# Attention scores of the mixing stage: one accumulation group a head, one mask product, rounded log-gate products of 384 columns

## The reference, cut to what matters

```python
# differential, per 128-query block
s = einsum('bqhcd,bkhcd->bhcqk', qi, k) * scale
p = softmax(where(causal, s, NEG_INF))
a = p[:, :, 0] - lam * p[:, :, 1]
# forgetting: logit[t,s] = q_t.k_s/sqrt(d) + sum_{s<j<=t} log f_j, causal
cum = cumsum(log_f, axis=1)
s = einsum('bqhd,bkhd->bhqk', qi, k) * scale + ci[..., None] - cum_k[:, :, None, :]
p = softmax(where(causal, s, NEG_INF))
```

## Time and profile before

| | |
|---|---|
| time, median of 3 runs | 2051.53 us (2051.78, 2051.53, 2048.94) |
| the profiled execution | 2050.4 us |
| its span, first to last instruction | 2048.3 us |
| TensorE busy | 1985.8 us (97%) |
| VectorE busy | 1429.2 us (70%) |
| ScalarE busy | 1147.7 us (56%) |
| mean granted TensorE clock | 0.993 |

### The profile page before, as it was taken

How to read it: one execution, slowest core, us unless ns; L and a number is a source line. 1 busy time by engine, 2 the same in 40 slices (tenths; PEclk the granted TensorE clock), 3 DMA queues, 4 the chain that set the end, 5 groups by cost and what they waited for, 6 DMA issues and landing times.

```text
span 2048.3 us, 33381 instructions
## 1 busy us (share of the span) xinstructions
PE 1985.8 (97%) x13864; PEld 1799.4 (88%) x13864; DVE 1429.2 (70%) x1902; ACT 1147.7 (56%) x1811; POOL 42.6 (2%) x32
## 2 busy tenths in 40 slices
PE   7999999999999999999999999999999999999999
PEld 7898798888989888888799987889989998878998
DVE  5456698898445778988856578765566657876555
ACT  6358745455435865554655565665565556566554
POOL 0100000000010000000001000000000100000000
PEclk9999999999999999999999999999999999999999
DMA  7353267996544236999555543245546554334553
GB/s 285 124 206 106 101 258 297 382 389 256 188 179 147 104 124 242 384 393 375 189 202 185 185 158 111 103 167 187 187 153 209 186 184 164 124 107 161 185 185 124
DMA packets 56165, 409.56 MB, mean 200 GB/s; under 512 B 6608, under 2 KB 6992, under 8 KB 7888
## 3 DMA queue, kind: packets, MB, share of 16 engines
q1 hardware_dynamic: 46512, 330.23, 45.2%
q10 hardware_dynamic: 9504, 77.21, 9.4%
HBM read 406.37 MB, written 1.05 MB: 199 GB/s over the span
## 4 chain that ended last, share of the span: by engine, by line
PE 81%; DVE 11%; ACT 5%; issue 2%; DMA 0%; POOL 0%; DVEq 0%; ACTq 0%; SPq 0%; POOLq 0%
PE bank L567 25%; PE bank L568 25%; PE bank L569 25%; DVE weights_low L392 3%; ACT weights_high L381 1%; DVE work L2311 1%; PE bank L949 1%; ACT weights_high L382 1%; PE bank L1906 1%; DVE work L523 1%; DVE h_low L534 1%; DVE work L1506 0%; DVE scratch L1501 0%; ACT work L435 0%; ACT work L436 0%
## 5 line engine op out<-in xcount | busy, mean ns | idle before, releaser
L392 DVE TENSOR_TENSOR weights_low<-raw_weights,weights_high 128x1024 fp32r<-128x1024 f32 x608 | 725.7, 1234 | 386.2 <-ACT weights_high L381 384.1
L567 PE MATMUL bank<-h_high,weights_high 128*128 128x256 f32 x3024 | 869.1, 287 | 17.6 <-DVE h_low L534 10.8
L568 PE MATMUL bank<-h_low,weights_high 128*128 128x256 f32 x3024 | 857.5, 284 | 0.0
L569 PE MATMUL bank<-h_high,weights_low 128*128 128x256 f32 x3024 | 857.2, 283 | 0.0
L381 ACT ACTIVATE weights_high<-raw_weights 128x1024 fp32r<-128x1024 f32 x304 | 321.6, 1058 | 631.3 <-PE bank L569 593.4
L567 PEld LDWEIGHTS bank<-h_high,weights_high 128*128 128x128 f32 x3024 | 581.6, 192 | 40.7 <-issue 17.0
L568 PEld LDWEIGHTS bank<-h_low,weights_high 128*128 128x128 f32 x3024 | 581.9, 192 | 2.6 <-issue 0.5
L569 PEld LDWEIGHTS bank<-h_high,weights_low 128*128 128x128 f32 x3024 | 581.8, 192 | 0.0
L382 ACT ACTIVATE weights_high<-raw_weights 128x1024 fp32r<-128x1024 f32 x304 | 317.5, 1044 | 0.0
L567 PE MATMUL bank<-weights_high,hidden_high 128*128 128x512 f32 x640 | 251.3, 393 | 1.8 <-DVE weights_low L392 1.8
L568 PE MATMUL bank<-weights_low,hidden_high 128*128 128x512 f32 x640 | 249.8, 390 | 0.0
(11 more groups left out here) (300 smaller groups left out, 1883.7 us busy)
## 6 DMA issues: line engine op xcount, KB each, us to landing
raw_weights<-in_stream SPq DMA_DIRECT2D x310, 1024.0 KB, 4.9
work<-in_ada ACTq DMA_DIRECT2D x64, 1152.0 KB, 9.2
consts<-in_consts SPq DMA_DIRECT2D x1, 2048.0 KB, 12.6
work<-in_row ACTq DMA_DIRECT2D x2, 836.0 KB, 5.1
x<-in_x SPq DMA_DIRECT2D x1, 1024.0 KB, 5.1
out_x<-x SPq DMA_DIRECT2D x4, 256.0 KB, 2.0
gain_row<-in_final SPq DMA_DIRECT2D x1, 512.0 KB, 13.2
vec<-in_vec SPq DMA_DIRECT2D x1, 169.0 KB, 12.5
```

The source lines that it names most:

```text
L392: dve.tensor_tensor(low[:, c], raw[:, c], high[:, c].bitcast(F32), ALU.subtract).then_inc(m.raw_done[plan.index[name] % RAW], 1)
L567: pe.matmul(out, aH, bH, start=start, stop=False, skip_group_check=True)
L568: pe.matmul(out, aH, bL, start=False, stop=False, skip_group_check=True)
L569: return pe.matmul(out, aL, bH, start=False, stop=stop, skip_group_check=True)
```

## The change

`mask_r` grows from two to five blocks of 128 columns; ScalarE fills the new three at the start with rounded copies of `tri_le`, `tri_le` and `ones`, both of which hold only 0 and 1. A new tensor `fox_r` of 16 columns holds the log gates as a rounded high part (8 columns) and a rounded low part (8 columns), written by two new VectorE instructions behind the one that used to signal `fox_lf`.

In `scores`, the product for the first block alone starts an accumulation; the q·k product of the second block follows at once and adds. The log gates of a fox task are added by four rounded products: for the high and then the low part, one of 384 columns (triangle, triangle, ones) and one of 128 columns. One rounded mask product per task covers both diagonal blocks (256 columns, every other block of 128 of the bank).

```diff
-        self.mask_r = sb("mask_rounded", 2 * P, F32R)
+        self.mask_r = sb("mask_rounded", 5 * P, F32R)
+        self.fox_r = sb("fox_rounded", 16, F32R)
...
-        def gate(i, tt):
-            return cols(m, FOX_LF + 4 * tt + i - FOX).to_broadcast([P, P])
+        def gate(i, tt, low):
+            at = 8 * low + 4 * tt + i - FOX
+            return m.fox_r[:, at:at + 1].to_broadcast([P, P])
 
         for i in tasks:
             q, k = qk(i)
             pe.matmul(score_bank(m, i)[:, 0:128], q[:, 0:128], k[:, 0:128], start=True, stop=False, skip_group_check=True)
+        for i in tasks:
+            q, k = qk(i)
+            add(score_bank(m, i)[:, 128:384], q[:, 128:256], k[:, 0:256])
         if first >= FOX:
             for i in tasks:
-                add(score_bank(m, i)[:, 0:128], gate(i, 0), m.const("tri_le"))
+                for low in range(2):
+                    add(score_bank(m, i), gate(i, 0, low), m.mask_r[:, 2 * P:5 * P])
+                    add(score_bank(m, i)[:, 256:384], gate(i, 1, low), m.mask_r[:, 2 * P:3 * P])
         for i in tasks:
-            add(score_bank(m, i)[:, 0:128], m.mask_r[:, 0:P], m.mask_r[:, P:2 * P], True)
-        for i in tasks:
-            q, k = qk(i)
-            pe.matmul(score_bank(m, i)[:, 128:384], q[:, 128:256], k[:, 0:256], start=True, stop=False, skip_group_check=True)
-        if first >= FOX:
-            for i in tasks:
-                s = score_bank(m, i)
-                add(s[:, 128:256], gate(i, 0), m.const("tri_le"), True)
-                add(s[:, 256:384], gate(i, 0), m.const("ones"))
-                add(s[:, 256:384], gate(i, 1), m.const("tri_le"))
-        for i in tasks:
-            add(score_bank(m, i)[:, 256:384], m.mask_r[:, 0:P], m.mask_r[:, P:2 * P], True).then_inc(m["scored"], 1)
+            add(tiles(score_bank(m, i), 3)[:, 0::2], m.mask_r[:, 0:P], wide(m.mask_r[:, P:2 * P], 2), True).then_inc(m["scored"], 1)
...
             dve.wait_ge(m["fox_l"], m.at("fox_l", 1))
-            dve.tensor_tensor(cols(m, FOX_LF, 8), cols(m, FOX_LF, 8), cols(m, FOX_L, 8), ALU.add).then_inc(m["fox_lf"], 1)
+            step(dve.tensor_tensor(cols(m, FOX_LF, 8), cols(m, FOX_LF, 8), cols(m, FOX_L, 8), ALU.add))
+            step(dve.tensor_copy(m.fox_r[:, 0:8], cols(m, FOX_LF, 8)))
+            dve.tensor_tensor(m.fox_r[:, 8:16], cols(m, FOX_LF, 8), m.fox_r[:, 0:8].bitcast(F32), ALU.subtract).then_inc(m["fox_lf"], 1)
             at_event(split_low, dve, m, plan, "ff")
...
+    for b, name in enumerate(("tri_le", "tri_le", "ones")):
+        act.activation(m.mask_r[:, (2 + b) * P:(3 + b) * P], m.const(name), ACT.Copy)
```

## The result

The changed kernel takes 2040.01 us (median of 5 runs, 2038.92 to 2041.27) against 2049.95 us for the kernel before (5 runs, 2048.94 to 2051.78): a ratio of 0.995, with a 95% interval of 0.9935 to 0.9964, so about 10 us or 0.5% faster. Its range ended at 2046.6.

What follows compares the result with a forecast made beforehand. TensorE, busy 97% of the span, was taken to bound the kernel only where it sets the end. First layer 1.45 us plus second 0.60 gave 2.05 off 2051.53: 2049.5 us, range 2046.6 to 2052.2.

Steps and rivals of the forecast that it cites:

- three rivals: Whole kernel: everything arrives, 2047.2 us (chance 0.14); nothing arrives, 2051.3 us (0.15); slower by the clock, 2058.5 us (0.09).
- Steps 0, 2 and 4: Scores ahead of line 1879, both layers: 0.31 us less each, all hidden behind VectorE, worth nothing.
- The score blocks: TensorE's scores: a block of differential tasks from 1.70 to 1.39 us, of fox tasks from 3.49 to 2.57.
- the q·k products: In each score block: 0.42 us for two of 128 columns plus 0.63 for those of 256.
- The gate products: In fox score blocks: 0.175 us for each rounded product of 384 columns, 0.12 for each of 128.
- the bound of 1.18: Upper bound in us of a fox block's saving: narrow gate products at 0.11, wide ones at 0.12.
- VectorE sets the turn of step 9: At line 1936, TensorE waits for VectorE's line 2480: 0.7 us in the first layer, over 1 in the second.
- The 0.40 us of the two new instructions: Added to VectorE's chain at step 6, second layer, 0.20 us each; in the first layer they disappear in idle time.
- First layer: Steps 6 to 9: of 1.23 us saved on TensorE, 0.53 arrive; 0.35 us of VectorE's idle time remain.
- Step 10: Scores for which VectorE waits 2.4 us: the fox block's 0.92 us arrive whole in each layer.
- The wait for the mixer's low half: Second layer, ahead of step 8's projection: part of TensorE waits for VectorE that sum to 1.5 us.
- The slow rival: New TensorE waits in steps 8 and 9 lower the clock: three times 3.0 us lost, 2058.5 us; chance 0.09.
- the signs named for being wrong: In the trace after: no wait at step 9's turn, a 384-column product over 0.23 us, a new slow clock stretch.

Runs made afterwards that it cites:

- pad400: Kernel before, with the mask tensor at 5 blocks and 16 unused columns behind it, so later tensors lie 1600 bytes further; 2041.82 us, ratio 0.9954.
- pad16: Kernel before, with 16 unused columns behind the mask tensor, so every later tensor moves by 64 bytes; 2042.62 us, ratio 0.9955.
- scores_old_addresses: Changed kernel with its new tensors allocated behind all others, so every old tensor has the address of before; 2048.13 us, ratio 0.9985.
- fox_split_late: `scores_old_addresses` with the two new VectorE log-gate instructions moved from step 5 to step 6; 2047.59 us, ratio 0.9984.
- scores_and_h_only: Changed kernel with 240 unused columns ahead of the hidden halves, putting them at a multiple of 512 bytes; 2031.51 us, ratio 0.9903.

## Why the prediction was wrong

**The step that failed is the list of what the change moves.** It said that transfers are untouched and that "no queue is passed by anything else", and took every product outside the scores at its old price. The grown mask tensor and the new one of 16 columns were read as bookkeeping. They are an edit of their own: they changed the distance between the operands of some 12,000 products. `pad400` puts 8.9 us on it. From the spacings of `pad16`: 8870 × 2.2 ns and 660 × 3.3 less, 1890 × 5.6 and 270 × 5.5 more (the last are products of 512 columns with the activations stationary), is 9.6 us less; measured are 8.1, and by the interval of the ratio 6 to 12. Nothing in the trace of before could have shown that price, but the edit itself was visible in the diff, and an unknown with that many instructions behind it belonged in the range, on both sides. None of the three rivals had it. Without it the time would have been 2048 us, inside the range.

**The rest of the sum held, in its total better than in its terms.** With the old addresses the change gave 2.5 us (1 to 5 us by the interval of the ratio, 0.9975 to 0.9995) where 2.05 were forecast. Point by point, from `scores_old_addresses`:

- Steps 0, 2 and 4 give nothing: from the first scores to line 1879 it is 38.1 us before and after, in both layers.
- The score blocks came out shorter than priced: 1.20 us for 1.39, and 2.33 for 2.57. The term that was too high is the q·k products: 0.42 + 0.63 when masks stood between them, but 0.85 in a row (1279.35 to 1280.20 above). I took two groups apart and added them unchanged. The gate products came at 0.225 to 0.28 for 384 columns and 0.058 for the 128 columns behind each, where I had 0.175 and 0.12; the sum of a pair, 0.28 to 0.34, is close to the 0.295 forecast, but both terms were wrong and made up for each other: that is luck. The saving of a fox block, 1.15 us, came near the bound of 1.18, which was reached by another way (gate products at their cheapest).
- VectorE sets the turn of step 9 in both layers: confirmed by `fox_split_late`. The 0.40 us of the two new instructions came as forecast in the second layer (10.2 to 10.6, turn 24.0 to 24.4).
- First layer: 25.2 became 24.4, where 24.65 was forecast. The forecast let 0.35 us of VectorE's idle time remain at step 6, and none was left (0.03). TensorE's shorter block of step 6, and 0.3 us by which it reached that step earlier in this profile (9.1 us behind line 1879's start instead of 9.4), brought the layer down to VectorE's own pace, which is why both layers now read 24.4.
- Step 10 arrives whole: 1.15 us shorter, VectorE's idle time ahead of its scores down from 2.43 us to 1.18, and the ends are 29.1 us behind the turn of step 9 instead of 30.2.
- The wait for the mixer's low half ahead of the projection of step 8 was foreseen, that the turn of step 8 itself waits for VectorE was not. It waits 0.46 us in the second layer with the old addresses, where the blocks alone are shorter than priced, and 0.84 and 0.80 us in the changed kernel, where the fill before it is faster too.

**The slow rival was seen once, in small.** Two of the signs named for being wrong came true in one layer: a slow stretch of the clock where none stood, and a turn of step 9 without a wait. (A third, a product of 384 columns over 0.23 us, holds for the first of a block, 0.28.) In the profile of the changed kernel, second layer, TensorE waits twice within two microseconds and then runs at the 1.2 GHz level:

```profile
1808.66 0.52 PE L1932 MATMUL bank<-consts,scratch 128*128 128x128 f32 x3 [0.80 <-DVE scratch L2474]
1809.99 0.58 PE L568 MATMUL bank<-weights_high,hidden_high 128*128 128x512 f32 x1 [0.81 <-DVE work L2383]
1810.37 0.63 PE L569 MATMUL bank<-weights_low,hidden_high 128*128 128x512 f32 x1
1810.80 0.63 PE L570 MATMUL bank<-weights_high,hidden_low 128*128 128x512 f32 x1
...
1813.95 0.39 PE L569 MATMUL bank<-weights_low,hidden_high 128*128 128x512 f32 x1
1814.18 0.40 PE L570 MATMUL bank<-weights_high,hidden_low 128*128 128x512 f32 x1
```

and the stretch from 1810 to 1814 us, with its busy times and, third from the end, the granted clock:

```profile
1810.00:1814.00 4.00, 4.00 (x11) 3.14 (x12) 3.10 (x11) 2.78 (x10) 0.00 (x0) 0.57 0.36 152
```

Products start 0.43 us apart instead of 0.23; from 1807 to 1810 us the granted clock had been 1.00. The turn of step 9 is at 25.6 instead of 24.4: 1.2 us lost. The prediction held this unlikely because each wait is short, and the rule of the Trainium skill that it set beside that (TensorE: Matmul & The Clock Gate, Why this matters for your kernels: no gaps over about 3 us) speaks of longer ones; here the clock fell after two of 0.8 us each. But the same two waits stand in the first layer of the same profile (0.84 and 0.81 us) and in the second layer of `scores_and_h_only`, where the turn of step 9 comes at 24.4:

```profile
1800.30 0.52 PE L1933 MATMUL bank<-consts,scratch 128*128 128x128 f32 x3 [0.86 <-DVE scratch L2475]
1801.63 0.47 PE L569 MATMUL bank<-weights_high,hidden_high 128*128 128x512 f32 x1 [0.81 <-DVE work L2384]
1801.93 0.39 PE L570 MATMUL bank<-weights_low,hidden_high 128*128 128x512 f32 x1
```

The granted clock stayed at 1.00 in both places. So these waits do not by themselves bring the clock down; what else was needed is not shown. It cost two fifths of the 3 us a stretch that I had priced.

What stays open: the mechanism behind the distances. That it is two reads of the same memory, the load of the stationary operand and the stream of the moving one, meeting in the same part of it, fits that only their distance counts and that the effect is there with TensorE alone. Load durations fit in one group (192 to 188 ns with the activations) and say nothing in the other (188 ns before and after with the hidden halves). It is argued, not shown; no run changed one read alone. Nor is it known why 660 token products prefer 64 bytes (114 to 117 ns) and the others 32.

## What to carry to other kernels

A change that adds or enlarges a tensor moves every tensor behind it; compare it with a run in which the old code has the new addresses, before its gain or loss is put down to the code. In a kernel that lives on dense rounded products, try pads of a few tens of bytes between the stationary and the moving operands: here that gave 8 to 19 us for no instruction at all, several times what the change of the scores gave, but 96 bytes on the activations gave nothing. Look at each shape by itself, since one can lose what another gains. And where TensorE's stream is shortened just ahead of a wait for another engine, look for that engine's own chain first: of 1.6 us that a layer's steps 6 and 8 became shorter with the old addresses, 0.8 arrived at the turn of step 9 in one layer and −0.4 in the other. With two tiny instructions taken off VectorE's chain it was 1.2 and nothing: where VectorE sets the pace, a shorter stream of TensorE gives nothing at all.

## What was not expected of the hardware

- Rounded products of 256 columns came at 116.8 to 120 ns, those of 512 at 227.7 to 233.4 ns, by the distance of their operands in SBUF, with what looks like a period of 256 bytes, at the same clock and with the same shapes. TensorE alone makes it.
- What helps one shape can hurt another: at 64 bytes the 256-column products gain 2.2 ns and the 512-column ones lose 5.6.
- A product of 384 columns followed by one of 128 costs 0.225 + 0.058 us. The narrow one costs half of an f32 record of 128 columns in a row (0.1125) and about half of a rounded mask product of 128 columns or less (0.11 to 0.17 up to the next full-row product). A reason that fits: its load starts behind the start of the wide product and 0.17 to 0.18 us ahead of the narrow product itself, so it runs while the wide one streams; no run tested it. The prediction weighed 0.12 against the Trainium skill's figure for an isolated product (TensorE: Matmul & The Clock Gate, Back-to-back issue gap): 56 ns at 128 columns. Behind a wide product the trace agrees with that figure (57 to 60 ns); no product in a row of narrow ones comes near it.
- Two q·k groups of 32 or 64 rows in a row cost 0.20 us less than the same with full-row products between them (0.85 against 0.42 + 0.63).
